# Linear attention: three reorderings around the context chunk's gate logits, the first unit's factors and the latents' sums

## What is computed

```python
def gla_chunk_scan(q, k, v, g, s0):          # chunks of 64 rows, 4 heads of 64 keys, 128 values
    b = jnp.cumsum(g, axis=2)
    b_mid, b_end = b[:, :, 31:32], b[:, :, -1:]
    att = einsum('bcthk,bcshk->bchts', q * exp(b - b_mid), k * exp(b_mid - b))
    o = einsum('bchts,bcshv->bcthv', where(tri, att, 0.0), v)
    ds = einsum('bcshk,bcshv->bchkv', k * exp(b_end - b), v)
    decay = exp(b_end[:, :, 0])              # s_start: state before each chunk, by a scan
    return o + einsum('bcthk,cbhkv->bcthv', q * exp(b), s_start)

g = log_sigmoid(lr[d] @ w2[d] + b[d]) / 16   # gate logits, rank 16, for direction d
for d, order in ((0, ident), (1, rev)):
    s_c = gla_final_state(k_ctx, v_ctx, g_ctx)   # the context only gives the first state
    o  += gla_chunk_scan(q_lat, k_lat, v_lat, g_lat, s_c)
cq_n, ckv_n = rms_norm(cq) * g_q, rms_norm(ckv) * g_kv
```

## Time and profile before

| | us |
|---|---|
| median of three runs | 2483.79 |
| their range | 2483.09 to 2490.51 |
| the profiled execution's own time | 2492.59 |
| its span | 2490.8 |
| PE busy in it | 2295.3 (92 %) |
| mean granted clock of PE | 0.953 |
| the stretch that the change touches, from the first `gq` chunk to the last read | about 1381 to 1659 |

### The profile page before, as it was taken

One profiled execution on the slowest core, in us unless ns is written; L12 is line 12 of the kernel. 1 busy time (PEld: TensorE's weight loads), 2 busy tenths in 40 slices (PEclk: granted clock), 3 DMA queues, 4 the chain that ended last, 5 costly groups with the idle time before them and its releaser, 6 DMA issues.

```text
span 2490.8 us, 27109 instructions
## 1 busy us (share of the span) xinstructions
PE 2295.3 (92%) x10870; PEld 1718.3 (69%) x10870; DVE 1525.6 (61%) x1882; ACT 1177.4 (47%) x1669; POOL 377.3 (15%) x272
## 2 busy tenths in 40 slices
PE   6999789798799999999979999998999998899998
PEld 5766465476388888888868777764555567688876
DVE  5776257534699999999873253436555547523475
ACT  3245246620288888888753232426444522412231
POOL 2000012000111111111100000010555633000014
PEclk9999899899899999999989987898999999899999
DMA  3201010114999999999862100130000032111131
GB/s 120 66 19 51 0 68 1 68 76 183 377 364 383 383 382 397 395 392 381 312 216 74 46 9 18 43 117 0 1 1 34 17 127 76 63 41 51 55 156 51
DMA packets 107420, 349.85 MB, mean 140 GB/s; under 512 B 23644, under 2 KB 55205, under 8 KB 79256
## 3 DMA queue, kind: packets, MB, share of 16 engines
q1 hardware_dynamic: 94856, 322.72, 34.7%
q0 software_dynamic: 11232, 21.09, 2.3%
q10 hardware_dynamic: 1200, 4.24, 0.4%
HBM read 327.38 MB, written 37.40 MB: 146 GB/s over the span
## 4 chain that ended last, share of the span: by engine, by line
PE 79%; DVE 13%; ACT 4%; issue 2%; DMA 2%; SPq 0%; POOL 0%; DVEq 0%; ACTq 0%; POOLq 0%
PE psm L230 75%; DVE small L3148 2%; DVE mem L959 1%; PE psm L1727 1%; DVE mem L1193 1%; DVE mem L2865 1%; DMA mem<-in_w_in_dram 1%; DVE r L343 1%; PE psm L1079 1%; PE psm L1750 1%; PE psm L470 1%; ACT mem L1149 1%; DMA mem<-in_odd_w_out_dram 1%; ACT mem L1115 0%; DMA mem<-h2d,small 0%
## 5 line engine op out<-in xcount | busy, mean ns | idle before, releaser
L230 PE MATMUL psm<-r,r 128*128 128x512 f32 (+3 forms) x7294 | 1762.8, 399 | 75.7 <-DVE r L343 18.0
L230 PEld LDWEIGHTS psm<-r,r 128*128 128x128 f32 (+2 forms) x7294 | 1369.2, 192 | 438.5 <-issue 72.2
L343 DVE TENSOR_TENSOR r<-mem,r 128x1024 fp32r<-128x1024 f32 (+1 forms) x456 | 527.1, 1203 | 141.1 <-ACT r L334 136.3
L334 ACT ACTIVATE r<-mem 128x1024 fp32r<-128x1024 f32 (+1 forms) x456 | 443.2, 1038 | 52.9 <-DMA mem<-in_w_in_dram 22.3
L230 PE MATMUL psm<-mem 128*64 128x128 f32 (+12 forms) x2230 | 370.9, 448 | 37.1 <-ACT mem L822 9.2
L230 PEld LDWEIGHTS psm<-mem 128*64 128x64 f32 (+6 forms) x2230 | 190.5, 178 | 174.5 <-issue 108.1
L3359 POOL TENSOR_TENSOR mem<-mem 128x1024 f32<-128x1024 f32 x63 | 152.6, 2422 | 167.1 <-ACT mem L3314 164.3
L3314 ACT ACTIVATE mem<-psm 128x512 f32<-128x512 f32 x160 | 94.5, 596 | 134.5 <-PE psm L230 127.5
L3148 DVE TENSOR_REDUCE small<-psm 128x1 f32<-128x1280 f32 x64 | 95.3, 1489 | 92.1 <-PE psm L230 92.0
L265 ACT ACTIVATE small<-small 128x1 f32<-128x1 f32 (+3 forms) x26 | 7.7, 295 | 236.7 <-DVE small L380 151.0
L230 PE MATMUL psm<-mem,cst 128*128 128x512 f32 (+5 forms) x220 | 85.4, 627 | 22.0 <-ACT mem L930 5.5
(11 more groups left out here) (339 smaller groups left out, 1744.3 us busy)
## 6 DMA issues: line engine op xcount, KB each, us to landing
mem<-in_exp_w_gate_dram SPq DMA_DIRECT2D x64, 1024.0 KB, 7.6
mem<-in_exp_w_up_dram SPq DMA_DIRECT2D x64, 1024.0 KB, 8.0
mem<-in_exp_w_down_dram SPq DMA_DIRECT2D x64, 1024.0 KB, 7.2
mem<-in_ada_w_dram SPq DMA_DIRECT2D x16, 1024.0 KB, 13.6
mem<-in_odd_w_in_dram SPq DMA_DIRECT2D x10, 1024.0 KB, 6.6
mem<-in_x_dram SPq DMA_DIRECT2D x16, 512.0 KB, 7.0
mem<-in_w_in_dram SPq DMA_DIRECT2D x8, 1024.0 KB, 5.4
mem<-in_ada_w_dram SPq DMA_DIRECT2D x16, 512.0 KB, 12.7
```

Of the source, the lines that this page charges most:

```text
L230: return p.e.matmul(o, l, r, start=start, stop=stop, skip_group_check=True)
L334: p.e.activation(h, mem(self.raw(i), [R * n])[:, w * q:w * q + w], ACT.Copy).then_inc(*self.hi_done.up(i, q))
L343: p.e.tensor_tensor(l, mem(self.raw(i), [R * n])[:, w * q:w * q + w], h.bitcast(F32), SUB).then_inc(*self.lo_done.up(i, q))
```

## The change

Three edits, none of which adds or removes work; PE's matmuls, DVE's and ACT's operations are the same ones in another order.

1. In the `gq` and `gk` 0 chunks the `norms` generators are advanced by two steps a chunk, not three.
2. In the first unit's `gla_ahead` generators PE makes the logits of chunk 0 one tile later, ACT and DVE handle them later, DVE sums the latents first, and DVE's factors and keys now stand ahead of its copy of the last `gk` chunk.
3. In the units' loop the logits of chunk 0 of the next unit are issued between the two reads, not ahead of both.

```diff
             for j in range(2):
-                WV.frees(4, by_channels_tensor(p, "gq", j, 4, 128 * j, 128, False, norms, 3))
-            by_channels_tensor(p, "gk", 0, 5, 0, 128, True, norms, 3)
+                WV.frees(4, by_channels_tensor(p, "gq", j, 4, 128 * j, 128, False, norms, 2))
+            by_channels_tensor(p, "gk", 0, 5, 0, 128, True, norms, 2)
...
             for j in range(2):
-                by_channels(p, who, "gq", j, 128, False, norms, 3)
+                by_channels(p, who, "gq", j, 128, False, norms, 2)
                 if j == 0:
                     split(p, 5)
-            by_channels(p, who, "gk", 0, 128, True, norms, 3)
+            by_channels(p, who, "gk", 0, 128, True, norms, 2)
             run(norms, 100)
...
         def gla_ahead_tensor(p):
 
-            for ch in (1, 2, 0):
+            for ch in (1, 2):
                 rise_tensor(p, 0, ch)
+            yield
+            rise_tensor(p, 0, 0)
             yield
 
         def gla_ahead_scalar(p):
             rise_scalar(p, 0, 1)
             rise_scalar(p, 0, 2)
+            yield
             rise_scalar(p, 0, 0)
-            yield
             factors_scalar(p, 0)
-            yield
             keys_scalar(p, 0)
             yield
...
             rise_min_vector(p, 0, 2)
             rise_sub_vector(p, 0, 2)
+            own_sums_vector(p, 0)
+            yield
             rise_min_vector(p, 0, 0)
             rise_sub_vector(p, 0, 0)
-            own_sums_vector(p, 0)
-            yield
             context_sums_vector(p, 0)
             differences_vector(p, 0)
-            yield
             factors_vector(p, 0)
             keys_vector(p, 0)
             yield
...
                 run(fill)
+                if k == 0:
+                    outputs_tensor(p, tau)
+                read_tensor(p, u, HALVES[k][0])
                 if u < 3:
                     rise_tensor(p, u + 1, 0)
-                if k == 0:
-                    outputs_tensor(p, tau)
-                for m in HALVES[k]:
-                    read_tensor(p, u, m)
+                read_tensor(p, u, HALVES[k][1])
                 run(fill)
```

## The result

| | before | after |
|---|---|---|
| median, us | 2485.46 (4 runs) | 2453.12 (4 runs) |
| range, us | 2483.09 to 2490.51 | 2449.97 to 2453.99 |
| profiled execution, us | 2492.59 | 2453.99 |
| its span, us | 2490.8 | 2452.2 |
| mean granted clock | 0.953 | 0.964 |

The ratio is 0.9863, with a 95 % interval of 0.9843 to 0.9884: faster by 32 us, 1.4 %, in the median. It lies inside the stated range, 9.5 us above the predicted 2443.6. Of the two profiled executions the changed one is 38.6 us shorter. The median before is of four runs, of which the prediction knew three; the profiled execution of the kernel before is none of them and lies above their range.

The account below looks back on a forecast made before the run. PE's stream was taken to bound the kernel, through idle time and low clock. Terms 35.1 + 0.9 + 0.86 + 1.6 + 1.7 = 40.2 us, taken from the median 2483.79, gave 2443.6; range 2434 to 2462.

Parts of the forecast that it names:

- The wait ahead of the reads: Ends of units 0 to 2: reads start without waiting for DVE's last state, at full clock; 35.1 us saved.
- unit 3's row: Unit 3's 96 read records, without a wait before them, took 9.83 us at full clock; taken as price for units 0 to 2.
- The margins of DVE's chain: Ends of units 0 to 2: `km` ready at 12.15 us after the fill, scores at 13.3, 1.1 us to spare.
- the 0.3 us at the weight split: Behind the first scores: PE newly waits 0.3 us for weight split L343, in units 0 and 1.
- Waits of 1.06 and 1.5 us: PE's remaining waits: about 1.06 us at the fifth latent sum, about 1.5 us at the first scores in place of 3.14.
- the latents' write: POOL's write, issued about 1422.5, lands by 1428.5; L2531 wants it at 1432.8, so hidden with 4 us to spare.
- From the profile to the median: Choice of base for the 40.2 us sum: profiled execution gives 2452.4, median 2483.79 gives 2443.6; the median was taken.
- one or two stretches still fall: Rival: one or two of three unit-end stretches still drop to 0.50, 9.2 us each; 2452.8 or 2462.0, chance 0.14.
- the clock belongs to the reads: Rival: all three unit-end stretches fall as before, whatever the wait; 26.9 us lost, 2470.5, chance 0.10.
- DVE was not late: Rival: chain to `km` takes 3 us longer, PE waits ahead of scores of units 1 to 3; 2454.7, chance 0.05.
- the slower case: Rival: clock falls in the reads and returns later, through two more rounds of scores and fill; 2496, chance 0.03.
- The bound of 24.9 us on the clock: Skill's rule of under 1 % ramp penalty: clock could give back at most 24.9 us, making the forecast 2447.3.

Follow-up runs that it names:

- The full wait put back: Changed kernel, with PE again waiting for DVE's last state before the first read of units 0, 1 and 2: 2481.55 us, ratio 0.9974.
- logits behind both reads: Changed kernel, with the next unit's context logits issued after both reads instead of between them: 2471.20 us, ratio 0.9933.
- edits 1 and 2: Kernel before with the first and second edit, without the third: 2480.41 us, ratio 0.9966.
- edit 3 alone: Kernel before with only the third edit, the next unit's context logits between the two reads: 2460.66 us, ratio 0.9885.
- edit 1: As a run: kernel before with the first edit alone: 2485.32 us, one run.
- edit 2: As a run: kernel before with the second edit alone: 2478.76 us, one run.
- best3: Changed kernel with two more waits removed, `kd` made behind the first masked copy, and half a fill between the next unit's two logit tiles: 2458.58 us, ratio 0.9874.

## Why the prediction was right, and where it was off

**The wait ahead of the reads, right.** Edit 3 was to remove 8.2 us of idle and 26.9 us of low clock. In the profiles it removed both in all three units: 36.2 us, against the profile that the prediction was made from, with the other edits and alone. The choice of unit 3's row as the price of reads at full clock, 9.8 us, held: 10.45 with the logits among them. The full wait put back brings the loss back in the median, and logits behind both reads show what DVE's chain costs when it is late. The sum had one price for such a wait, though, and one of 2.73 us, put back, had no fall behind it. One reading was loose: in the profile that the prediction was made from the falls came 1.8, 1.5 and 0.9 us into the work behind the waits, not about 2, and in the profile of edits 1 and 2 one came 0.6 us before unit 0's wait was over.

**The margins of DVE's chain, right.** The timeline of DVE in the changed kernel, at the end of unit 0:

```profile
1473.05 2.64 DVE L2865 SCALAR_TENSOR_TENSOR mem<-mem,small,psm 128x128 f32<-128x128 f32 x7
1479.01 0.48 DVE L2510 TENSOR_SCALAR mem<-psm,small 128x256 f32<-128x256 f32 x1 [3.32 <-ACT mem L2495]
...
1483.56 1.22 DVE L2592 TENSOR_TENSOR mem<-mem 128x1024 f32<-128x1024 f32 x1
...
1486.09 1.29 DVE L343 TENSOR_TENSOR r<-mem,r 128x512 fp32r<-128x512 f32 x2
```

`km` is there at 1484.78, 1.5 us ahead of the scores at 1486.31, where 1.1 was forecast. DVE's operations take the same times as before (2.64, 0.48, 1.22, 1.29 us), though PE's clock beside them is now the full one. Of the 0.3 us at the weight split little shows: it ended at 1487.38, and PE's next fill began at 1487.44, 1.13 us after the scores, against 1.09 in unit 3.

**Edits 1 and 2, right, with luck in one term.** Waits of 1.06 and 1.5 us were forecast, 0.99 and 1.04 came; the 0.86 us went. L2531 did not wait for the latents' write, which was issued at 1423.89, 10.5 us ahead of L2531's start at 1434.37. None of the ten profiles with edit 2 has a stretch at 0.50 between the first latent sum and unit 0's logit pair, so both went, where one was counted. The second was not a sure gain: without edit 2 it stands in two profiles of four.

**From the profile to the median, wrong.** This is the step that failed. The sum, made against the profiled execution, gave 2452.4, within 1 us of the measured 2453.12. I then subtracted it from the median, 2483.79, and forecast 2443.6. I had said that I could not see where the 8.8 us between that profile and the median lay; the subtraction holds only if they lie outside the stretches that the change removes. They did not, as far as a second profile shows: it is 9.4 us shorter in span, has 10.7 us less in the stretch of the change and one long stretch at 0.50 fewer. What a run had already saved there the change could not save again. Against the first profile the stretch of the changed kernel is 41.4 us shorter, against the second 30.8; the medians moved by 32.3. For edit 3 alone the two are 35.0 and 24.4, and the median moved by 26.7.

That 2452.4 came so close is in part luck. The unit ends gave 36.2 us where 35.1 was counted, the way to the first scores 5.3 for 5.1, the second short stretch 1.6 that was not counted, and a new short stretch took 1.6 back; outside the stretch the changed kernel's profile is 2.8 us longer, which nobody had forecast.

**The rivals.** That one or two stretches still fall did not happen in either profile of the changed kernel. The reason that I gave for it, a mix of logits and a short wait, may act elsewhere: the new stretch of 3.4 us at 1509.3 stands behind the logit pair of unit 1 and 0.20 us of wait, costing 1.6 us. That the clock belongs to the reads is out: after the change they hold 1.00 in all three units. DVE was not late, and the slower case found nothing for it.

The bound of 24.9 us on the clock was worked out from a sentence of the Trainium skill ("TensorE: Matmul & The Clock Gate", Part 1, "What's actually happening") which puts the penalty of the ramp under 1 % of a typical kernel's span. Less idle time explains 12.2 of the 41.4 us by which the stretch shrank against the first profile, which leaves 29.2 for the clock, above the bound; against the second profile it is 10.6 of 30.8, which leaves 20.2, below it. So these runs do not decide about the bound. The mean granted clock of 0.953 before shows only that the low clock takes more than 1 % of this span. The 2447.3 worked out by the bound was taken from the median too, and missed 2453.12 by the same step.

## What to carry to other kernels

When work with few columns and rows per matmul follows a wait of PE, price the wait by what stands behind it: in the profile with all three long stretches 2.6 us idle ahead of 10 us of small matmuls cost 12 us, while 3.5 us idle ahead of scores and fills of full matmuls cost 5.7 (17.2 in three places, between the medians). That is a price that such a wait can have, not one that it always has: one of 2.73 us cost little more than itself (16.2 us from fill to scores, against 13.2). Look for work that does not need the thing waited for and issue it first, and then check the chain that hangs on what was put back: here it had 1.5 us to spare between the reads and was 3.5 us late behind them. And when a sum removes something that comes and goes between executions, make it against the profiled execution and compare with the expected time from there; subtracting it from the median can count the same saving twice. If there is time for one more profile of the kernel before, take it: the two here differ by 10.7 us in the stretch of the change.

## What the runs showed of the hardware that was not expected

- A short stretch at the low clock can save a long one. Of the 15 unit ends in the five profiles with the old order at the unit ends (the kernel before twice, edit 1, edit 2, edits 1 and 2), four had 3.4 us at 0.50 early in the unit, then a wait of 1.06 to 1.12 us and reads at 1.00. Fill's end to next scores took 14.5 us in the one shown, against 25.2. The other eleven had waits of 2.63 to 3.01 us and 17.1 to 23.9 us at 0.50.
- The clock fell for 3.4 us in the fill behind a pair of K = 16 matmul tiles of 2 us with a wait of 0.20 us ahead of them. It did so in unit 1 in both profiles of the changed kernel (1509.3 in the first), and in 10 of 26 places in all: units 0 and 1 of the 13 profiles with the pair unsplit. It fell at the 0.86 us wait in four profiles of four; it did not fall behind 1.96 us between full matmuls, also in four of four. What decides between the 10 and the other 16 is not shown.
- Reads (matmuls of 128x128 and 64x64) hold the full clock for 10.45 us in the changed kernel, and for 10.53 us behind a wait of 2.73. Once the clock had fallen at or in them, it did not come back before they ended, in row lengths of 16.8 to 18.8 us; one fall that had begun in the fill ahead of them (best3) ended 0.7 us into them.
